# State-space mixer of a two-block model: four tile preparations in another order, one copy on another engine, six loads on another queue

## What is computed

```python
def ssd_chunked(xs, dt, A, Bm, Cm):
    """Mamba-2 SSD with chunked scan.
    xs (B,S,H*P), dt (B,S,H), A (H,), Bm/Cm (B,S,G*N) -> (B,S,H*P) float32."""
    f32 = jnp.float32
    B_, S_, _ = xs.shape
    nc = S_ // CHUNK
    G, Hg, P, N = SSD_GROUPS, SSD_HEADS_PER_GROUP, SSD_HEAD, SSD_STATE
    x = xs.astype(f32).reshape(B_, nc, CHUNK, G, Hg, P)
    dt = dt.reshape(B_, nc, CHUNK, G, Hg)
    Bc = Bm.astype(f32).reshape(B_, nc, CHUNK, G, N)
    Cc = Cm.astype(f32).reshape(B_, nc, CHUNK, G, N)
    a_dt = dt * A.reshape(G, Hg)
    a_cs = jnp.cumsum(a_dt, axis=2)
    xdt = x * dt[..., None]

    seg = a_cs[:, :, :, None] - a_cs[:, :, None, :]
    tril = jnp.tril(jnp.ones((CHUNK, CHUNK), dtype=bool))[None, None, :, :, None, None]
    decay_in = jnp.exp(jnp.where(tril, seg, -jnp.inf))
    cb = jnp.einsum('bclgn,bcsgn->bclsg', Cc, Bc)
    y_diag = jnp.einsum('bclsgh,bcsghp->bclghp', cb[..., None] * decay_in, xdt)

    decay_st = jnp.exp(a_cs[:, :, -1:] - a_cs)
    states = jnp.einsum('bcsgn,bcsghp->bcghpn', Bc, xdt * decay_st[..., None])
    chunk_decay = jnp.exp(a_cs[:, :, -1])

    def step(h, inp):
        s_c, d_c = inp
        return h * d_c[..., None, None] + s_c, h

    h0 = jnp.zeros((B_, G, Hg, P, N), f32)
    _, prev = lax.scan(step, h0, (jnp.moveaxis(states, 1, 0), jnp.moveaxis(chunk_decay, 1, 0)))
    prev = jnp.moveaxis(prev, 0, 1)
    y_off = jnp.einsum('bclgn,bcghpn->bclghp', Cc, prev) * jnp.exp(a_cs)[..., None]
    return (y_diag + y_off).reshape(B_, S_, SSD_WIDTH)
```

## Time and profile before

| | |
|---|---|
| median of 3 runs | 3650.99 us (3645.95 to 3656.31) |
| the profiled execution | 3650.99 us, of which the span from the first to the last instruction is 3649.2 us |
| busy, share of the span | PE 74%, weight loads 53%, DVE 59%, ACT 16%, POOL 36% |
| mean granted TensorE clock | 0.858 |
| DMA | 1006.31 MB, mean 276 GB/s |

### The profile page before, as it was taken

The page is one execution under the profiler, slowest core; times in us unless marked ns, Lnnn a source line. Parts: engine busy times, 40 slices in busy tenths (PEclk is TensorE's granted clock), DMA queues, the critical chain, the costliest instruction groups (busy, mean ns, idle before and its releaser), DMA issues. The chain is left out here.

```text
span 3649.2 us, 44644 instructions
## 1 busy us (share of the span) xinstructions
PE 2696.2 (74%) x17746; PEld 1944.6 (53%) x17746; DVE 2141.9 (59%) x3992; ACT 587.5 (16%) x1213; POOL 1315.4 (36%) x1082
## 2 busy tenths in 40 slices
PE   5977433657992066799975657799999789777787
PEld 4867323555430055688863546578888567322232
DVE  5543898878776987999987988333222443100001
ACT  1031001210000012222222200132222321100001
POOL 0000258567776766677764656200000000000000
PEclk7989667778996578799987778989999889889998
DMA  7613579689999989799998799523332325899997
GB/s 272 237 35 116 192 265 390 216 322 380 357 366 376 379 310 351 274 397 399 395 341 276 251 364 353 185 69 108 99 100 85 116 93 195 334 428 428 428 428 321
DMA packets 390750, 1006.31 MB, mean 276 GB/s; under 512 B 30381, under 2 KB 234515, under 8 KB 375699
## 3 DMA queue, kind: packets, MB, share of 16 engines
q0 software_dynamic: 150912, 549.52, 40.3%
q1 hardware_dynamic: 211856, 406.65, 30.3%
q10 hardware_dynamic: 27779, 47.38, 3.6%
HBM read 971.99 MB, written 31.46 MB: 275 GB/s over the span
## 5 line engine op out<-in xcount | busy, mean ns | idle before, releaser
L1427 POOL DMA_INDIRECT ring<-in_peer_u_dram,index x512 | 683.7, 1335 | 435.8 <-DVE ring L1505 198.4
L1427 POOL DMA_INDIRECT ring<-in_peer_v_dram,index x512 | 602.5, 1177 | 294.4 <-DVE h_rows_b L1511 135.9
L345 PE MATMUL bank<-hT,weights 128*128 128x256 f32 x2240 | 505.2, 389 | 175.7 <-DMA weights<-in_w_in_dram 84.3
L345 PEld LDWEIGHTS bank<-hT,weights 128*128 128x128 f32 x2240 | 436.9, 196 | 243.3 <-issue 103.8
L1821 PE MATMUL bank<-hT,weights 128*128 128x256 f32 x1792 | 420.8, 389 | 4.0 <-DVE weights L2019 4.0
L1821 PEld LDWEIGHTS bank<-hT,weights 128*128 128x128 f32 x1792 | 336.4, 192 | 54.2 <-DVE weights L2019 4.4
L1505 DVE SCALAR_TENSOR_TENSOR ring<-ring,h_rows_a 128x1024 f32<-128x1024 f32 x256 | 304.7, 1221 | 64.4 <-DMA ring<-in_peer_u_dram,index 62.4
L1511 DVE SCALAR_TENSOR_TENSOR h_rows_b<-ring,coef,h_rows_b 128x1024 f32<-128x1024 f32 x238 | 305.1, 1282 | 46.9 <-DMA ring<-in_peer_v_dram,index 27.9
L1505 DVE SCALAR_TENSOR_TENSOR ring<-ring,h_rows_b 128x1024 f32<-128x1024 f32 x256 | 299.8, 1224 | 5.0 <-DMA ring<-in_peer_u_dram,index 4.5
L2838 POOL IOTA mo_down<- 128x4 f32 x1 | 0.1, 144 | 789.6 <-POOLq L160 789.6
L1524 PE MATMUL bank<-ring,weights 128*128 128x512 f32 x512 | 223.3, 597 | 9.3 <-DVE weights L1499 9.0
(11 more groups left out here) (562 smaller groups left out, 4097.8 us busy)
## 6 DMA issues: line engine op xcount, KB each, us to landing
weights<-in_w_in_dram SPq DMA_DIRECT2D x112, 512.0 KB, 3.9
weights<-in_w_in_dram SPq DMA_DIRECT2D x54, 1024.0 KB, 9.7
xp_near<-in_w_exp_gate_dram SPq DMA_DIRECT2D x9, 4096.0 KB, 33.7
xp_far<-in_w_exp_up_dram SPq DMA_DIRECT2D x9, 4096.0 KB, 33.0
xp_near<-in_w_exp_up_dram SPq DMA_DIRECT2D x7, 4096.0 KB, 33.9
xp_far<-in_w_exp_gate_dram SPq DMA_DIRECT2D x7, 4096.0 KB, 35.7
xp_near<-in_w_exp_down_dram SPq DMA_DIRECT2D x7, 4096.0 KB, 34.5
xp_far<-in_w_exp_down_dram SPq DMA_DIRECT2D x7, 4096.0 KB, 32.8
```

Of the source, the lines that this page charges most:

```text
L345: ins = pe.matmul(m.ps[b][:, 0:TH], m.weights[:, s, k, c * P:(c + 1) * P], rhs(k), start=(k == 0), stop=(k == k_tiles - 1))
L1427: pool.indirect_dma_start(out=self.ring[:, n % RING, :], out_offset=None, in_=self.tables[table], in_offset=bass.IndirectOffsetOnAxis(ap=s ...
```

## The change: what it does

- `load_tiles` (six loads of 512 KB) is issued from ScalarE's queue, as its first instructions in the small block, ahead of its wait for the small inputs and its exp; SP issues only the last weight slot. ScalarE's wait for the loads stays at its end.
- The copy of bank 4 into `bt` goes from ScalarE to VectorE; `bt_kept` goes.
- VectorE's order in each chunk: `xdt` 0, `xdts` 0, `xdt` 1, `xdts` 1, `xdt` 2, `xdts` 2, `xdt` 3, `xdts` 3, `bt`, `cb`, instead of four `xdt`, `cb`, four `xdts`. Each `xdts` waits for the `xdt` just ahead of it.
- TensorE waits once, ahead of the first spreading of a chunk, for all of these (14 counts), instead of for the banks that it is about to overwrite.

```diff
--- before.py
+++ after.py
@@ -2388,7 +2388,7 @@
         eng.wait_ge(self.landed, 80)
 
 
-def ssd(m, half, p, few, load_tiles, tiles_landed, up, state, more=None):
+def ssd(m, half, p, few, load_tiles, up, state, more=None):
 
     nc = m.nc
     assert SN * SG == KT
@@ -2408,7 +2408,6 @@
 
             @block.sync
             def _(sp):
-                load_tiles(sp)
                 up.load(sp, SLOTS - 1, SLOTS)
 
             @block.tensor
@@ -2431,6 +2430,7 @@
 
             @block.scalar
             def _(act):
+                tiles_landed = load_tiles(act)
                 few.wait(act)
                 act.activation(small[:, 2:3], small[:, 1:2], ACT.Exp).then_inc(soft, 1)
                 act.wait_ge(soft, 3)
@@ -2444,7 +2444,7 @@
                 act.activation(left[:, :, :], left[:, :, :], ACT.Exp).then_inc(soft, 1)
                 act.activation(whole[:, :, :], whole[:, :, :], ACT.Exp).then_inc(soft, 1)
                 up.keep(act, 1)
-                tiles_landed(act)
+                tiles_landed()
 
             @block.vector
             def _(dve):
@@ -2481,7 +2481,6 @@
         dec = sb("sd_dec", [P, 2, GH, SC])
         inn = sb("sd_inn", [P, 2, GH, SC])
         names = ("x_turned", "rows_kept", "spread", "exps", "seg", "scores", "y_made", "y_kept", "s_made", "s_kept")
-        bt_kept = m.sem("sd_bt_kept_n")
         x_turned, rows_kept, spread, exps, seg_made, scores, y_made, y_kept, s_made, s_kept = (
             m.sem(f"sd_{x}_n") for x in names)
         h3 = lambda ap: ap.rearrange("p (h c) -> p h c", c=RH)
@@ -2513,11 +2512,10 @@
                         ins = pe.matmul(m.ps[5][:, g * P:(g + 1) * P], p[:, S_TILES + g, t], p[:, S_TILES + SG + g, t],
                                         start=True, stop=True)
                     ins.then_inc(x_turned, 1)
+                    pe.wait_ge(rows_kept, 14 * (n + 1))
                     for g in range(SG + 1):
                         if g < SG:
                             i = n * SG + g
-                            if g < 2:
-                                pe.wait_ge(rows_kept, 9 * n + 2 * g + 2)
                             if i >= 2:
                                 pe.wait_ge(exps, 3 * (i - 1))
                             for h in range(GH):
@@ -2532,7 +2530,6 @@
                             gp = g - 1
                             bank = m.ps[4 + i % 2]
                             pe.wait_ge(scores, 2 * (i + 1))
-                            pe.wait_ge(bt_kept, n + 1)
                             if i >= 2:
                                 pe.wait_ge(y_kept, 4 * (i - 1))
                             for h in range(GH):
@@ -2554,8 +2551,6 @@
             @block.scalar
             def _(act):
                 for n in range(SN):
-                    act.wait_ge(x_turned, 6 * n + 5)
-                    act.copy(bt[:, :, :].rearrange("p g s -> p (g s)"), m.ps[4][:, :]).then_inc(bt_kept, 1)
                     for g in range(SG):
                         i = n * SG + g
                         if i >= 2:
@@ -2600,26 +2595,27 @@
                 for n in range(SN):
                     if n:
                         dve.wait_ge(y_kept, 4 * SG * n)
-                    k4 = lambda ap: ap.rearrange("p (k h c) -> p k h c", k=2, c=RH)
-                    wide = lambda ap, b: (ap[:, n, b * GH:(b + 1) * GH].rearrange("p (k h) -> p k h", k=2)
-                                          .unsqueeze(3).to_broadcast([P, 2, GH // 2, RH]))
                     for b in range(4):
+                        q = slice(b * 512, (b + 1) * 512)
+                        k4 = lambda ap: ap.rearrange("p (k h c) -> p k h c", k=2, c=RH)
+                        wide = lambda ap: (ap[:, n, b * GH:(b + 1) * GH].rearrange("p (k h) -> p k h", k=2)
+                                           .unsqueeze(3).to_broadcast([P, 2, GH // 2, RH]))
+                        x2 = xdt[:, 2 * b:2 * b + 2]
                         dve.wait_ge(x_turned, 6 * n + b + 1)
-                        dve.tensor_tensor(xdt[:, 2 * b:2 * b + 2], k4(m.ps[b][:, :]), wide(tok[:, 0], b),
-                                          ALU.mult).then_inc(rows_kept, 1)
+                        dve.tensor_tensor(x2, k4(m.ps[b][:, :]), wide(tok[:, 0]), ALU.mult).then_inc(rows_kept, 1)
+                        dve.wait_ge(rows_kept, 14 * n + 2 * b + 1)
+                        dve.tensor_tensor(k4(xdts[:, q]), x2, wide(left), ALU.mult).then_inc(rows_kept, 1)
+                    dve.wait_ge(x_turned, 6 * n + 5)
+                    dve.tensor_copy(bt[:, :, :].rearrange("p g s -> p (g s)"), m.ps[4][:, :]).then_inc(rows_kept, 1)
                     dve.wait_ge(x_turned, 6 * n + 6)
                     dve.tensor_tensor(cb[:, :, :], m.ps[5][:, :].rearrange("p (g l) -> p g l", l=SC),
-                                      m.upto[:, :].unsqueeze(1).to_broadcast([P, SG, SC]), ALU.mult).then_inc(rows_kept, 1)
-                    for b in range(4):
-                        dve.wait_ge(rows_kept, 9 * n + b + 1)
-                        dve.tensor_tensor(k4(xdts[:, b * 512:(b + 1) * 512]), xdt[:, 2 * b:2 * b + 2], wide(left, b),
-                                          ALU.mult).then_inc(rows_kept, 1)
+                                      m.upto[:, :].unsqueeze(1).to_broadcast([P, SG, SC]), ALU.mult).then_inc(rows_kept, 5)
                     for g in range(SG):
                         i = n * SG + g
 
                         beside(m, dve, 5.0)
                         dve.wait_ge(exps, 3 * (i + 1))
-                        dve.wait_ge(rows_kept, 9 * (n + 1))
+                        dve.wait_ge(rows_kept, 14 * (n + 1))
                         d = dec[:, i % 2]
                         dve.tensor_tensor(d, d, cb[:, g, :].unsqueeze(1).to_broadcast([P, GH, SC]),
                                           ALU.mult).then_inc(scores, 1)
@@ -2671,22 +2667,20 @@
     nc = m.nc
     y_landed = m.sem("sd_x_landed")
 
-    def load_tiles(sp):
+    def load_tiles(act):
         for g in range(X_TILES // 4):
-            sp.dma_start(y[:, 4 * g:4 * g + 4, :],
+            act.dma_start(y[:, 4 * g:4 * g + 4, :],
                           projected[S_TILES + 4 * g:S_TILES + 4 * g + 4].rearrange("k p t -> p k t")).then_inc(y_landed, 16)
-
-    def tiles_landed(act):
-        act.wait_ge(y_landed, 16 * (X_TILES // 4))
+        return lambda: act.wait_ge(y_landed, 16 * (X_TILES // 4))
 
     n0 = norms_at["norm_g"]
     with ExitStack() as own:
         if half.first:
-            ssd(m, half, y, few, load_tiles, tiles_landed, up, state)
+            ssd(m, half, y, few, load_tiles, up, state)
             gate = OutGate(m, half, own, y, projected, then)
         else:
             gate = OutGate(m, half, own, y, projected, then)
-            ssd(m, half, y, few, load_tiles, tiles_landed, up, state, gate.load_z)
+            ssd(m, half, y, few, load_tiles, up, state, gate.load_z)
         up.done()
         return group_norm(m, lambda n: y[:, n, :], lambda n: y[:, n, :], norms[:, n0:n0 + S_TILES], SG, S_TILES // SG,
                           False, D // 2, first=gate, scaled=scaled)
```

## The result

The changed kernel takes 3683.55 us (median of 10 runs, 3672.91 to 3691.86) against 3657.17 us before (median of 10 runs, 3645.95 to 3665.22): a ratio of 1.0067, 95% interval 1.0054 to 1.008, or 24.5 us more (20 to 29). Part of that gap is that the kernel before itself was 6 us slower over ten runs than over the three that the forecast started from; by the ratio alone, 3651 would have become 3675.5, inside the range. The profiled execution has a span of 3680.3 us, 31.1 us above the one before.

The account below looks back on a forecast made before the run. The prediction took ScalarE's wait for tile landing (first half) and the chain to TensorE's second up-projection tile (second), then spreading and exps, as bounds. Terms 8.4 + 2.6 + 5.0 + 2.0 = 18.0 us, taken as +17 on 3651: 3668 us (3659 to 3677).

Parts of the forecast that it names:

- the sum: Added cost of order and wait plus loads, both halves: 8.4 + 2.6 + 5.0 + 2.0 = 18.0 us.
- The order and the wait, second half: Main block: spreading waits for ten VectorE instructions, 4.2 us later in each of two chunks; +8.4 us (5.0 to 10.8).
- The same in the first half: Main block, order and wait: +2.6 us (1.6 to 4.0). Small block, loads: issues hidden, landing later, +2.0 us (0 to 2.9).
- The six loads on ScalarE, second half: Small block: issues delay ScalarE's exp and the chain to the second up-projection tile; +5.0 us (0.8 to 8.5).
- The rule that was weighed: Second half's loads: another issuing engine saves only small sequencer time, so shared landing alone costs 1.8 us instead of 5.0.
- Chain hidden, transfers only: Rival for the loads: ScalarE issues in 3.0 us and clocks hold; 14.4 us, 3665 us; chance 0.2.
- the pause only moves: Rival for the main blocks: TensorE pauses before the spreading, y runs at 2.4 GHz; 8.9 us, 3660 us; chance 0.17.
- Slower still: Rival for both blocks: all restarts at half clock, fifth and sixth issues blocked; +26, 3677 us; chance 0.12.
- Faster: Rival, first half's small block: tiles overtake gathers and weights, at best -6.2 us; chance 0.06, 0.03 of it faster.
- the sign that the prediction named for being wrong: First half's small block: the tiles land earlier than before.

Follow-up runs that it names:

- e1: The changed kernel with the six tile loads back on SP, ahead of the last weight slot; ratio 1.004, 14.6 us slower than the kernel before.
- e3: The changed kernel with loads on SP, TensorE waiting for counts 3 and 7 of 14 before spreading groups 0 and 1, all 14 before y; ratio 1.0006.
- e6: The kernel before with the six loads on ScalarE and the last weight slot's load moved to the start of the main block; ratio 1.0018.
- e2: The kernel before with only the six tile loads moved to ScalarE's queue; ratio 1.0036, 13 us slower.
- e7: The kernel before with the six tile loads on ScalarE, but behind its first exp instead of ahead of it; ratio 1.004.
- e5: The kernel before with tile loads 0 to 3 on ScalarE and 4 and 5 on SP, ahead of the last slot; ratio 1.0016.
- e11: The kernel before with the tile loads on ScalarE as three of 1 MB instead of six of 512 KB; one run, 3659.42 us.
- e4: The kernel before with TensorE waiting for all nine counts ahead of the spreading of groups 0 and 1; ratio 1.0028, 10.2 us slower.

## Why the prediction was right or wrong

Stage by stage, the main blocks came near the forecast (11.9 us measured by the windows, 11.0 in the sum), and the small blocks did not: 15.2 us against 7.0. So what failed are the two terms of the six loads on ScalarE, one in its size, the other in what it called hidden.

**The order and the wait, second half.** Right in mechanism: spreading 6.65 us after the first `xdt` (6.67 worked out), a pause of 4.05 us, half clock behind it. The sum said 8.4 us (5.0 to 10.8); measured 10.1 in the change and 7.9 in e1. I had taken the clock's loss and gain as of one size. The gain did not come: y still ran at 0.50. Only the loss stayed, 1.1 us in chunk 0 (13.08 - 7.84, less the 4.12 us by which the spreading started later). And the price that I gave to the new order belongs to the single wait: with waits by bank the same order is free (e3).

**The same in the first half.** +2.6 us forecast, +1.8 measured in the change and +3.5 in e1. This block's length varies by 1.7 us without any edit (128.8 to 130.5), so the rows inside it say more, and they came as worked out: from the first `xdt` to L2620 it is 0.6 us less in chunk 0 (12.19 against 12.83; 0.3 less was forecast), where lookup steps fill the wait, and 2.5 us more in chunk 1 (2.9 more was forecast).

**The six loads on ScalarE, second half.** This is the step that failed in size: "The issues cost at least 0.38 + 5 x 0.53 = 3.0 us ... and 6.1 us by what SP took for the same six". They cost 9.28 us. The mechanism held (L2457 released by ScalarE, the chain late, the shared landing hidden, half clock in the second tile: 4.95 us), and the term of 5.0 us (0.8 to 8.5) measured 9.0 us. SP's 6.1 us were no upper bound: they are from a queue that had the DMA engines to itself in that stretch (108.1%), while ScalarE's queue had 45% of them beside the weights on SP's. With 1.0 MB less beside them the six took 6.00 us (e6). That an issue waits for room in its own queue is what these amounts suggest; no run shows it alone.

**The same in the first half.** "The chain has 6.5 us of cover there (1978.63 to 1985.14), so the issue time is hidden". This step was wrong, and not only in size: 13.87 us of issues pushed L2457 9.9 us later (from 5.6 to 15.5 us into the block), and the second up-projection tile took 6.10 instead of 3.67 us behind the longer pause; 9.9 + 2.4 - 6.5 is 5.8 of the 6.2 us. I had carried the 4 us of the second half over to a stretch in which the gathers share the queues as well. +2.0 forecast, +6.2 measured, with ScalarE's chain, not the landing, at the end.

**The rule that was weighed.** By it the sum would have been 3.2 us less. The measurement decides against it here: the issues held ScalarE for 9.28 and 13.87 us, and its chain, not the landing, ended both small blocks (e2, 13 us). The Trainium skill, DMA: Bandwidth & Descriptors, section Issuing engines are not separate DMA queues, says that the time on the sequencer to initiate a DMA is usually small beside the DMA itself; in this case it was not. The interleaving that the same section of the Trainium skill states is what the trace shows: 22% of the engines' time for ScalarE's queue, 22% for SP's and 56% for the gathers while the first six issues stood.

**The rivals.** "Chain hidden, transfers only" and "the pause only moves" are refuted by L2457's releaser and the windows. "Slower still" named both causes that came (restarts at half clock, blocked issues), had 3677 us and 0.12, and was the nearest: its sum was 26 us, the windows' 27.1. "Faster", the overtaking tiles: in the first half ScalarE's queue had moved all but two packets of the tiles by 1987 us, 21 us into the block, where the kernel before waited for them for 22.9 us. That is the sign that the prediction named for being wrong, and the gain it stands for did not come, because ScalarE's last copy ended more than 7 us later still.

## What to carry to other kernels

Count a DMA issue as work of the engine that issues it, and do not take its length from another queue: the same six took from 6.00 to 13.87 us on ScalarE, by what else was moving. Put loads on an engine that has nothing else to do before the data is used, and look at whose chain stands behind them. When several waits are merged into one, the cost is the end of the last instruction waited for minus that of the one that was needed (4.1 us for each chunk here), not the work that was added, and the clock behind the pause comes on top (1.1 us here); the order that cost nothing measurable behind fine waits (e3) cost 14.6 us behind a single one (e1). And a wait for all loads at a block's end can be split by user: that was the one gain here, 4.7 us, just clear of noise.

## What the runs showed of the hardware

Six issues of 512 KB on ScalarE returned when 0.95 to 1.64 MB of their 3.15 MB had moved, in both halves of after, e2, e6 and e7 (DMA queue rows over the time of the issues, for ScalarE's queue q10). After, first and second half, and e6_slot_later's second half:

```profile
q10 hardware_dynamic: 1113, 1.11, 22.3%
```

```profile
q10 hardware_dynamic: 1404, 1.41, 44.8%
```

```profile
q10 hardware_dynamic: 1384, 1.39, 66.1%
```

Their times were 13.87, 9.28 and 6.00 us. So the sixth issue on this queue returned with about 2 MB (1.5 to 2.2 MB) still to move, and its time fell as the share of the engines that the queue got rose: 22%, 45% and 66%. The four of e5 returned with 2.0 and 1.8 MB to move, but the three of 1 MB in e11 with 2.3 and 2.6 MB, so one fixed amount does not fit all of them. With packets of 1 KB on this queue beside gathers with packets of 3.6 KB in the mean (3.08 MB in 849 packets in the first stretch, against 1.11 MB in 1113), the queue with the small packets got the fewer bytes. That it is room in the queue, counted in bytes, in packets or otherwise, rather than some other limit, is read from these amounts and not shown by a run of its own.

Behind pauses of 3.2 us (e4) to 4.1 us (after, e1) ahead of it, the spreading's 32 records took 5.4 to 7.2 us instead of 3.83, at the 1.2 GHz level for part of them (clock 0.50 in the window of after). The same pause had two prices in two executions, 6.47 us in e1 and 7.19 us after, and two in one: 5.37 and 6.83 us in the two chunks of e4.
